# First layer's filter taps moved from the start of the kernel to behind the first projection chunk

## The reference, cut to what matters

```
mod = SiLU(cond) @ w_mod + b_mod                 # 6 rows of 1024 for context and for latent
h = x * (1 + scale1) + shift1
proj = h @ w_in                                  # the "first projection", 1696 columns
# Hyena filters, from positions and weights alone, not from x:
hid  = sin(freq0 * (z @ w1 + b1)); hid = sin(freq1 * (hid @ w2 + b2))
filt = (hid @ w3) * exp(-t * deltas)             # the taps: (L, 2 orders, 2 directions, 256)
two_sided = concat(fwd, 0, bwd[:0:-1]); k_spec = rfft(two_sided)
```

## Time and profile before

| | |
|---|---|
| Time, three runs | median 1057.02 us (1051.01, 1057.02, 1060.02) |
| The profiled execution | 1051.0 us, span 1049.2 us |
| PE busy | 953.4 us, 91% of the span |
| DVE, ACT, POOL busy | 555.9, 342.3, 91.2 us |
| Chain that ended last | PE 72%, DVE 12%, DMA 11% |
| DMA | 305.02 MB, mean 291 GB/s |

### The profile page before, as it was taken

The page is one execution under the profiler, slowest core; times in us unless marked ns, Lnnn a source line. Parts: engine busy times, 40 slices in busy tenths (PEclk is TensorE's granted clock), DMA queues, the critical chain, the costliest instruction groups (busy, mean ns, idle before and its releaser), DMA issues.

```text
span 1049.2 us, 15187 instructions
## 1 busy us (share of the span) xinstructions
PE 953.4 (91%) x5824; PEld 513.4 (49%) x5824; DVE 555.9 (53%) x1271; ACT 342.3 (33%) x725; POOL 91.2 (9%) x90
## 2 busy tenths in 40 slices
PE   3899998999989999999799998799999999998982
PEld 1565676554544444443236667565454443444431
DVE  5624315785674353544468454486674354443547
ACT  2221012461224433433333213264223443433331
POOL 0250000100320000000007000000220000000000
PEclk9999999999999999999989999999999999999987
DMA  9979999504297999999938224011279799999961
GB/s 318 421 284 385 416 386 379 208 22 160 118 378 308 399 422 420 421 419 421 421 129 349 63 83 164 1 61 59 123 306 399 314 422 420 421 420 421 420 285 62
DMA packets 47506, 305.02 MB, mean 291 GB/s; under 512 B 5971, under 2 KB 6228, under 8 KB 14644
## 3 DMA queue, kind: packets, MB, share of 16 engines
q1 hardware_dynamic: 40524, 275.67, 64.6%
q0 software_dynamic: 6208, 26.06, 6.8%
q10 hardware_dynamic: 688, 2.17, 0.7%
HBM read 298.93 MB, written 4.95 MB: 290 GB/s over the span
## 4 chain that ended last, share of the span: by engine, by line
PE 72%; DVE 12%; DMA 11%; issue 2%; ACT 2%; DVEq 1%; SPq 0%; ACTq 0%
PE bank L1080 19%; PE bank L963 8%; PE bank L1183 6%; PE bank L1059 6%; PE bank L797 6%; DMA ring<-in_moe_gate_up 4%; PE bank L776 4%; DMA ring<-in_w_mod 3%; PE bank L808 3%; PE bank L698 3%; DMA region_k<-in_moe_down 2%; PE bank L906 2%; PE bank L849 2%; PE bank L680 2%; PE bank L952 1%
## 5 line engine op out<-in xcount | busy, mean ns | idle before, releaser
L963 PE MATMUL bank<-ring,act_t 128*128 128x512 f32 x192 | 84.1, 594 | 0.0
L1528 ACT ACTIVATE arena<-bank 128x384 f32<-128x384 f32 x64 | 31.2, 490 | 134.9 <-PE bank L1059 134.7
L1059 PE MATMUL bank<-sel,h_hi 128*128 128x384 f32 x192 | 69.2, 361 | 3.6 <-DVE sel L2111 3.6
L1080 PE MATMUL bank<-ring,arena 128*32 128x512 f32 x480 | 58.2, 602 | 8.9 <-DMA ring<-in_moe_gate_up 5.5
L1059 PE MATMUL bank<-sel,h_lo 128*128 128x384 f32 x192 | 64.8, 338 | 0.0
L963 PEld LDWEIGHTS bank<-ring,act_t 128*128 128x128 f32 x192 | 35.8, 190 | 43.6 <-issue 43.6
L1059 PEld LDWEIGHTS bank<-sel,h_hi 128*128 128x128 f32 x192 | 36.0, 187 | 36.7 <-issue 30.6
L797 PE MATMUL bank<-act_t,ring 128*128 128x384 f32 x160 | 52.3, 487 | 0.0
L1080 PE MATMUL bank<-arena 128*32 128x512 f32 x384 | 47.8, 599 | 3.3 <-DVE arena L2143 3.3
L1183 PE MATMUL bank<-y_hi,selT 128*128 128x512 f32 x108 | 46.7, 433 | 0.0
L776 PE MATMUL bank<-ring,act_t 128*128 128x256 f32 x192 | 44.1, 391 | 2.5 <-DVE act_t L1755 2.5
(11 more groups left out here) (356 smaller groups left out, 1787.4 us busy)
## 6 DMA issues: line engine op xcount, KB each, us to landing
ring<-in_moe_gate_up SPq DMA_DIRECT2D x60, 1024.0 KB, 10.8
region_k<-in_moe_gate_up SPq DMA_DIRECT2D x40, 1024.0 KB, 10.2
ring<-in_w_mod SPq DMA_DIRECT2D x33, 1024.0 KB, 9.6
ring<-in_moe_down SPq DMA_DIRECT2D x32, 1024.0 KB, 11.6
arena<-in_moe_down SPq DMA_DIRECT2D x28, 1024.0 KB, 11.1
arena<-in_moe_gate_up SPq DMA_DIRECT2D x16, 1024.0 KB, 11.1
ring<-in_w_in SPq DMA_DIRECT2D x9, 1024.0 KB, 14.8
ring<-in_w_out SPq DMA_DIRECT2D x8, 1024.0 KB, 5.0
```

What stands on the lines that cost most here:

```text
L963: mm = pe.matmul(ps[2 * t + half][:, :], act_t[:, 2 * c + k, t * P:(t + 1) * P], w[:, k, half * 512:(half + 1) * 512], start=(c == 0 and k ...
L1059: mm = pe.matmul(ps[gather_bank(o, k)][:, 0:TOK], src[:, t, k * P:(k + 1) * P], sel[:, t, :, :].rearrange("p v n -> p (v n)"), start=(t == ...
L1080: return pe.matmul(out[r, :], stationary[:, r], moving, start=start, stop=stop, tile_position=(0, UNIT * j), skip_group_check=True)
L1528: act.activation(xg[:, first:first + VISITS, k, :], ps[gather_bank(o, k)][:, 0:TOK].rearrange("p (v n) -> p v n", n=P), ACT.Copy)\
```

## The change

PE issues all eight chunks of group 0 in one go. The first layer's taps follow the first projection chunk: tile 0, two `w_mod` chunks of `FILL[0]`, tile 1, the other two, tile 2. Ahead of tiles 1 and 2 PE waits until DVE has finished the tile before (`filt_eo`), since all tiles now share the banks 3, 4 and 5. The wait for `filt_eo` ahead of the transposes goes. On DVE `filter_taps(0)` moves from ahead of `add_group(0)` to between the two halves of `filter_hidden` of layer 1. No load, matmul or elementwise operation is added or taken away.

```diff
-TAP_BANKS = ((0, 1, 2, 3, 4, 5), (4, 5, 6, 7, 3, 4))
+TAP_BANKS = ((3, 4, 5, 3, 4, 5), (4, 5, 6, 7, 3, 4))
@@ PE, filter_taps
             for t in tiles:
                 if l > 0 and t == 2:
                     pe.wait_ge(s["filt_eo"], at("filt_eo", l, 1))
+                if l == 0 and t > 0:
+                    pe.wait_ge(s["filt_eo"], t)
@@ PE, start
-        mod_sums(MOD_START[:3])
-        filter_taps(0)
-        mod_sums(MOD_START[3:])
+        mod_sums(MOD_START)
         pe.wait_ge(s["cst_in"], 48)
@@ PE, layer loop
-            if l == 0:
-                pe.wait_ge(s["filt_eo"], at("filt_eo", 0))
-            else:
+            if l > 0:
                 filter_taps(l, (0,))
@@ PE, behind the first projection chunk
                 if c == 0:
-                    fill(l, 0)
                     if l == 0:
+                        filter_taps(0, (0,))
+                        mod_sums(FILL[0][:2])
+                        filter_taps(0, (1,))
+                        mod_sums(FILL[0][2:])
+                        filter_taps(0, (2,))
                         filter_hidden(1, 1)
@@ DVE, layer loop
                 filter_hidden(1, 0)
+                filter_taps(0)
                 filter_hidden(1, 1)
```

## The result

| | before | changed |
|---|---|---|
| Time, first comparison | 1054.01 us median (1050.91 to 1060.02, 4 runs) | 1064.54 us median (1063.63 to 1065.53, 4 runs) |
| Ratio | | 1.0099, 95% interval 1.0071 to 1.0127 |
| Time, repeated later | 1053.68 us median (1050.12 to 1060.02, 23 runs) | 1065.01 us median (1064.05 to 1065.82, 6 runs) |
| Ratio | | 1.0114, 95% interval 1.0092 to 1.0135 |
| Span of the profiled execution | 1049.2 us | 1061.7 us |

The changed kernel is slower by about 11 us, and its runs lie within 2 us where those of before spread over 9 to 10.

The account below looks back on a forecast made before the run. Bound: the weight stream to 35.59 us, then PE from 43.54 through the spectra, with the stream's next issue behind them. 12.6 us plus 1.1 for the clock, 13.7, on median 1057.02 gave 1070.7 us; range 1061 to 1079.

Parts of the forecast that it names:

- The start gains nothing: Up to 43.5 us: removing the taps from beneath the weight DMA gains 0; the eighth chunk stays last to land.
- my own sign: Stated sign of being wrong: the part before 43.5 us moves by more than 3 us.
- POOL's anchor: Tile 0's end: POOL's last operation sets it, so a PE start 2.7 us later moves it only 1.2.
- the second rival: At the start: dft, issued earlier, pushes the eighth chunk's landing back by up to 2.7 us; total 1075, chance 0.22.
- Six tap matmuls on PE's chain, 5.4 us: Behind projection chunk 0: six tap matmuls, 1.8 us a tile, stand on PE's chain with no cover.
- PE's stands, 0.9 to 1.0 us a tile, without POOL: Ahead of tiles 1 and 2: PE waits for filt_eo, 4.5 us after a tile's start, against 3.6 of work.
- DVE held by POOL, +5.3 us: In tile 0: lines 1791 and 1792 wait for POOL's operations; filt_eo rises 9.8 us after PE's start, not 4.5.
- The second stand: Ahead of tile 2: PE stands about 1 us waiting for tile 1's filt_eo.
- the clock term of 1.1: In the fill after PE's stand: work at 1.2 GHz costs between 0 and 1.7 us, taken as 1.1.
- SP's wait, 13 us longer: At the spectra: they end at about 92 to 94 us in place of 79.4, and SP's wait grows 13 us.
- No meeting with POOL: Rival: POOL ends by about 58 us, before tile 0's line 1791, so 5.3 us fall away; 1064.3 us, chance 0.20.
- Not on the path: Rival: landed stream data or the DMA step at 162.59 absorbs the added time; total stays 1057, chance 0.05.

Follow-up runs that it names:

- the repeat: The changed kernel run and profiled once more, unedited, beside more runs of before: ratio 1.0114 to before.
- a_ series: Profiles of the changed kernel, unedited (two), with dft issued later, or with useless start matmuls: chunk 0 at 43.58 to 47.46 us; totals 1064 to 1070 us.
- b_idle_fill: Kernel before, with six useless 128x512 matmuls in the fill behind projection chunk 0: ratio to before 1.0049.
- a_pool_late: Changed kernel, with POOL's six layer-norm operations of layer 0 held until DVE has done both halves of layer 1's filter_hidden: 1064.9 us (2 runs).
- b_warm: Kernel before, with three useless 128x512 matmuls ahead of the first weight chunk: median 1051.5 us, ratio to before 0.9979.
- b_warm_spectra: Kernel before, with three useless matmuls ahead of the first weight chunk and layer 0's spectra behind chunk 0's fill: median 1050.7 us, ratio 0.9970.
- a_dft_six: Changed kernel, with POOL issuing the dft load when six weight chunks are used up in place of five: 1068.9 us (2 runs).
- b_spectra_early: Kernel before, with layer 0's spectra moved from behind projection chunk 1 to behind chunk 0's fill: 1052.38 us, ratio to before 0.9988.

## Why the prediction was right or wrong, point by point

- *The start gains nothing.* Right, and more: it lost 3.0 us (46.58 against 43.54), which I had put at 0, with +3 as the bound for the clock and +1.2 for `dft`. 0.3 are a later stream, 1.2 the eighth chunk's landing behind `dft`, 0.9 its sums and 0.7 the transposes at 1.2 GHz. Both mechanisms were named; the value taken was too low. By my own sign, a part before 43.5 that moves by more than 3 us, I stand on the edge: it moved by 3.0, and by 3.9 in the repeat. That this did not make the kernel slower still is POOL's anchor: the a_ series has tile 1 at 65 to 66.6 wherever chunk 0 starts.
- *`dft` and an idle DVE.* That its packets would start sooner beside an idle DVE, as the second rival had it, didn't show: DVE does nothing from 24.4 to 39.2 in the changed kernel, and the first packets come 3.8 us behind the issue (30.77, 34.6) where it was 3.7 before (32.43, 36.1).
- *Six tap matmuls on PE's chain, 5.4 us.* Right: 5.5 alone (b_idle_fill). In the changed kernel the three tiles take 5.8.
- *PE's stands, 0.9 to 1.0 us a tile, without POOL.* Right: 0.79 twice in a_pool_late.
- *DVE held by POOL, +5.3 us.* The mechanism was right, as a_pool_late shows by taking it away; the size was not. `filt_eo` 1 came at 65.9 (predicted 65.65), but 7.0 us behind tile 0's start and not 9.8, so the term is +2.5. PE came to tile 0 3 us later and POOL's operations 1.0 us earlier (49.62 against 50.64), and two tap operations were held, for 0.84 and 2.57 us, where I had three. The stand of PE was 3.37 us and not 6: the start's loss was spent from the stand.
- *The second stand.* It didn't occur: at 1.2 GHz the fill took 3.46 us for its half, and PE was later than DVE. From tile 1 to tile 2 it was 5.44 us where I had 4.55; this 0.9 is what the clock term of 1.1 amounted to.
- *The sum, 13.7 us.* Measured to the spectra's end, 13.9 (15.5 in the repeat). The parts, in the changed kernel: start 3.0; taps 5.8; stand 3.4; fill at 1.2 GHz 1.7. In my sum they were 0, 5.4, 7.2 for the two stands, and 1.1. That start and stands make up for each other is the anchor, which I had described; that the whole agrees to 0.2 us is luck.
- *SP's wait, 13 us longer.* Wrong: it was 23.1 us against 20.4, 2.7 longer. Its end moved by 13.9, but I had left out its beginning: SP issues first into the slots that the second half of the fill frees, and that half stands behind tile 1 now (`region_w` issued at 69.92 in place of 58.62).
- *The time, 1070.7 us.* 6 us too high, and below the range that I gave the forecast itself, 1067 to 1075.5. I added the sum to the median of three runs, 1057.02, and more runs of before put that at 1053 to 1054. And before's median can hold executions in which its own start loses 6 us, a loss that the changed kernel, without taps there, can't have: against the 1051 of an execution with the taps at 2.4 GHz the difference is 1065.0 - 1051.0 = 14.0, against the median of b_warm 13.5, against before's own 11. How much of before's median that loss makes is inferred from times and not shown, and b_warm_spectra warns that it need not reach the end whole. I had read the spread of 9 us as noise and looked for no cause.
- *The chances.* Slower by over 1% had 0.70; the two ratios are 1.0099 and 1.0114, on that bound, so on which side of it the result fell is luck.
- *The rivals.* The stream's eighth chunk pushed back did happen (1.2 us), without the total it was given, since the anchor took it up. No meeting with POOL was given 1064.3, and that is the time that was measured: by the number alone it would have won. The trace excludes it, with DVE held and PE standing 3.37 us; when it is brought about in a_pool_late, chunk 1 starts 5.1 us earlier, 1.7 of them clock. Not on the path: excluded by b_idle_fill.

## What to carry to other kernels

Work that fits beneath a DMA wait is free, and moved behind it, it is paid in full; ask of each place which wait ends last there before moving something to a "quieter" one. A wait that ends at a time set by a third party, here POOL's operations, swallows gains ahead of it, and in a_dft_six the gain became a loss, with a longer stand of PE and a longer stretch at 1.2 GHz behind it. When runs of one kernel spread by more than its neighbour's, compare the starts in several profiles: part of the spread may be something that can be mended, here by three matmuls of no use. And a total that agrees with a forecast, or with a rival, proves neither: compare the terms.

## What of the hardware I had not expected

- At the start of an execution the same code ran its taps in 5.4 us or in 10.5 to 10.6, though PE had summed the same three chunks before. In b_spectra_early the granted clock reads 1.00 over that stretch, so the durations show 1.2 GHz where the column doesn't:

```profile
25.00:30.00 5.00, 5.00 (x14) 1.97 (x7) 2.25 (x6) 1.27 (x2) 0.00 (x0) 1.00 1.01 426
30.00:35.00 5.00, 5.00 (x8) 1.87 (x6) 4.61 (x13) 0.00 (x0) 0.00 (x0) 1.00 1.01 423
```

- After PE had stood 5.64 us in a_dft_six, the clock stayed at 0.50 for over ten us of work that kept PE busy 4.97 of 5 and 6.00 of 6 us:

```profile
65.00:70.00 5.00, 4.97 (x18) 1.76 (x22) 2.66 (x7) 0.00 (x0) 1.21 (x3) 0.50 0.66 249
70.00:76.00 6.00, 6.00 (x29) 1.96 (x21) 2.01 (x6) 0.00 (x0) 0.00 (x0) 0.50 0.49 175
```

In the changed kernel, after a stand of 3.37 us, it reads 0.95, 0.50, 0.70 and 1.00 in the four windows of 2 us from 66 on. Why it stayed low for longer in the one was not tried.
